# Router logits in one decoder layer: high and low weight parts as one 72-column stationary operand, product in three pieces

## What is computed

```
x = LN(alpha*x + mix)                                   # 512 x 1024
g_logit = x @ rg_w + rg_b                               # 4 groups
e_logit = x @ re_w + re_b                               # 32 experts, 8 to a group
group   = argmax(softmax(g_logit))
top 2 of the 8 experts of that group, weights renormalised, times the group's probability
y = sum over the chosen experts of  (silu(x @ gate) * (x @ up)) @ down
x = LN(alpha*x + y);  x = x + sigmoid(x @ W_g) * (p @ W_p)
```

## Time and profile before

| | us |
|---|---|
| median of 3 runs | 634.6 |
| the three runs | 635.39, 634.60, 633.86 |
| the profiled execution, its own time | 636.33 |
| its span, first to last instruction | 634.6 |
| PE busy | 602.2 (95%) |
| DVE busy | 353.9 (56%) |
| ACT busy | 182.5 (29%) |
| POOL busy | 170.6 (27%) |
| moved by DMA | 149.88 MB, mean 236 GB/s |

### The profile page before, as it was taken

The page is one execution under the profiler, slowest core; times in us unless marked ns, Lnnn a source line. Parts: engine busy times, 40 slices in busy tenths (PEclk is TensorE's granted clock), DMA queues, the critical chain, the costliest instruction groups (busy, mean ns, idle before and its releaser), DMA issues.

```text
span 634.6 us, 11747 instructions
## 1 busy us (share of the span) xinstructions
PE 602.2 (95%) x4575; PEld 435.4 (69%) x4575; DVE 353.9 (56%) x857; ACT 182.5 (29%) x360; POOL 170.6 (27%) x191
## 2 busy tenths in 40 slices
PE   8999999999999999998899999996699999978997
PEld 6768979878888778887665555564465555535885
DVE  6799994788787677869562113221111221129855
ACT  5587324344243245202101111110011111234221
POOL 2428772001010011512033332343233343111100
PEclk9999999999999999999799999997999999989999
DMA  7503241013004001399959999999999999977003
GB/s 245 220 31 150 84 170 63 1 47 154 1 2 164 36 1 68 124 390 395 380 226 367 368 418 416 420 413 421 413 418 416 416 418 415 421 307 313 0 3 135
DMA packets 29286, 149.88 MB, mean 236 GB/s; under 512 B 5993, under 2 KB 6457, under 8 KB 15273
## 3 DMA queue, kind: packets, MB, share of 16 engines
q1 hardware_dynamic: 23624, 140.65, 55.6%
q0 software_dynamic: 5600, 8.42, 3.7%
HBM read 145.23 MB, written 12.98 MB: 249 GB/s over the span
## 4 chain that ended last, share of the span: by engine, by line
PE 75%; DMA 10%; DVE 9%; issue 3%; ACT 1%; POOL 1%; SPq 0%; DVEq 0%; ACTq 0%
PE bank L2318 13%; PE bank L1945 12%; PE bank L1947 12%; PE bank L1946 12%; PE bank L2374 7%; DMA rows_x<-in_ple_gate_dram 5%; DMA slots<-in_w_exp_dram 4%; PE bank L2334 3%; PE bank L2308 2%; PE bank L2050 2%; PE bank L2065 2%; PE bank L2078 2%; PE bank L2351 1%; PE bank L2108 1%; DMA raw<-in_w_in_dram 1%
## 5 line engine op out<-in xcount | busy, mean ns | idle before, releaser
L1847 DVE COPY rows_x<-bank 128x128 f32<-128x128 f32 (+1 forms) x41 | 11.0, 267 | 175.5 <-PE bank L2366 99.9
L1945 PE MATMUL bank<-w_hi,a_hi 128*128 128x384 f32 (+1 forms) x240 | 88.2, 367 | 1.7 <-DVE a_lo L1601 1.7
L1947 PE MATMUL bank<-w_hi,a_lo 128*128 128x384 f32 (+1 forms) x240 | 86.5, 361 | 0.0
L1946 PE MATMUL bank<-w_lo,a_hi 128*128 128x384 f32 (+1 forms) x240 | 86.5, 360 | 0.0
L1945 PE MATMUL bank<-a_hi,w_hi 128*128 128x512 f32 x152 | 61.4, 404 | 1.0 <-DVE w_lo L1241 0.7
L1946 PE MATMUL bank<-a_lo,w_hi 128*128 128x512 f32 x152 | 59.4, 391 | 0.0
L1947 PE MATMUL bank<-a_hi,w_lo 128*128 128x512 f32 x152 | 59.4, 391 | 0.0
L852 POOL DMA_INDIRECT pair_dram<-rows_x,row_put x26 | 26.4, 1015 | 101.0 <-ACT rows_x L1152 101.0
L1945 PEld LDWEIGHTS bank<-w_hi,a_hi 128*128 128x128 f32 x240 | 45.2, 188 | 7.0 <-DVE a_lo L1601 2.1
L1152 ACT ACTIVATE rows_x<-bank 128x512 f32<-128x512 f32 (+1 forms) x41 | 21.3, 520 | 94.9 <-PE bank L2374 72.8
L2318 PE MATMUL bank<-raw,rows_x 128*64 128x256 f32 x416 | 47.8, 383 | 0.5 <-DVE rows_x L1816 0.5
(11 more groups left out here) (320 smaller groups left out, 1141.8 us busy)
## 6 DMA issues: line engine op xcount, KB each, us to landing
raw<-in_w_exp_dram SPq DMA_DIRECT2D x45, 1024.0 KB, 17.9
slots<-in_w_exp_dram SPq DMA_DIRECT2D x24, 1024.0 KB, 23.7
pa<-in_w_exp_dram SPq DMA_DIRECT2D x21, 1024.0 KB, 17.4
raw<-in_w_in_dram SPq DMA_DIRECT2D x18, 512.0 KB, 3.5
raw<-in_w_wide_dram SPq DMA_DIRECT2D x4, 1536.0 KB, 6.9
raw<-in_w_out_dram SPq DMA_DIRECT2D x4, 1024.0 KB, 5.9
rows_x<-in_w_exp_dram SPq DMA_DIRECT2D x4, 1024.0 KB, 15.0
raw<-pair_dram SPq DMA_DIRECT2D x8, 512.0 KB, 9.2
```

Source lines behind the costliest of these rows:

```text
L1945: t_.matmul(o, lh, rh, start=first, stop=False)
L1946: t_.matmul(o, lh, rl, start=False, stop=False)
L1947: return t_.matmul(o, ll, rh, start=False, stop=last)
```

## The change

The high and the low part of the router's weights stand side by side for each block of rows, so that one stationary operand has 72 columns. One product with `a_hi` gives high x high in rows 0 to 35 and low x high in rows 36 to 71; one with `a_lo` adds high x low and low x low. So each block takes two products instead of three. The two halves of the 72 rows are added on DVE after the transposes. The product is made in three pieces, of tokens 0 to 255, 256 to 383 and 384 to 511, each in a PSUM bank of its own, and in each piece the eight products with `a_hi` come before the eight with `a_lo`, with waits by half tile. Four idle products of 512 columns stand between the first and second piece. low_first(1) moves on DVE from ahead of mixed(3, 1) to behind norm_centre(3).

```diff
-        logit_rows = take(SEQ)[0:36, :]
+        logit_rows = take(SEQ)[0:72, :]
-        WR_N = NK * 36
+        wr_two = last_lo[:, 0:NK * 72].rearrange("p (k c) -> p k c", k=NK)
+        logit_bank = [bank[4], bank[0], bank[5]]
+        LOGIT_COLS = [slice(0, 2 * P), slice(2 * P, 3 * P), slice(3 * P, 4 * P)]
...
-                sp.wait_ge(s_rp, 2)
+                sp.wait_ge(s_rp, 3)
...
-            def copy_logits(half):
-                act.wait_ge(s_rp, half + 1)
-                c = slice(half * 2 * P, (half + 1) * 2 * P)
-                a.activation(logit_rows[:, c], bank[4][0:36, c], ACT.Copy).then_inc(s_ra, 1)
+            def copy_logits(i):
+                act.wait_ge(s_rp, i + 1)
+                c = LOGIT_COLS[i]
+                a.activation(logit_rows[:, c], logit_bank[i][0:72, 0:c.stop - c.start], ACT.Copy).then_inc(s_ra, 1)
...
-                    a.activation(last_lo[:, 0:WR_N], wr_raw.rearrange("p k c -> p (k c)"), ACT.Copy)\
-                        .then_inc(s_wrs, 1)
+                    a.activation(wr_two[:, :, 0:36], wr_raw, ACT.Copy).then_inc(s_wrs, 1)
                 if u == 5:
                     copy_logits(0)
             copy_logits(1)
+            copy_logits(2)
...
             norm_scale(2, s_ln, s_rs)
-            low_first(1)
             mixed(3, 1)
             norm_centre(3, s_ln)
+            low_first(1)
             norm_scale(3, s_ln, s_rs)
             low_first(2)
             low_first(3)
...
-            step(v.tensor_tensor(logit, bank[0][:, 0:NT * 36].rearrange("p (t c) -> p t c", t=NT),
-                                 r_bias.unsqueeze(1).broadcast_to([P, NT, 36]), ALU.add))
+            turned_logits = bank[1][:, 0:NT * 72].rearrange("p (t w c) -> p t w c", t=NT, w=2)
+            step(v.tensor_tensor(logit, turned_logits[:, :, 0, :], r_bias.unsqueeze(1).broadcast_to([P, NT, 36]),
+                                 ALU.add))
+            settle()
+            step(v.tensor_tensor(logit, turned_logits[:, :, 1, :], logit, ALU.add))
...
-            def route(half):
-                pe.wait_ge(s_x1lo, 4 * half + 4)
-                c = slice(half * 2 * P, (half + 1) * 2 * P)
+            def route_high(i):
+                c = LOGIT_COLS[i]
                 for k in range(NK):
-                    mm = three(bank[4][0:36, c], wr_hi[:, k, :], wr_lo[:, k, :], a_hi[:, k, c], a_lo[:, k, c],
-                               k == 0, k == NK - 1)
+                    if k % 4 == 0:
+                        pe.wait_ge(s_x1hi, (i + 1) * 2 + 1 + k // 4)
+                    t_.matmul(logit_bank[i][0:72, 0:c.stop - c.start], wr_two[:, k, :], a_hi[:, k, c], start=k == 0,
+                              stop=False)
+
+            def route_low(i):
+                c = LOGIT_COLS[i]
+                for k in range(NK):
+                    if k % 4 == 0:
+                        pe.wait_ge(s_x1lo, (i + 1) * 2 + 1 + k // 4)
+                    mm = t_.matmul(logit_bank[i][0:72, 0:c.stop - c.start], wr_two[:, k, :], a_lo[:, k, c],
+                                   start=False, stop=k == NK - 1)
                 mm.then_inc(s_rp, 1)
...
             pe.wait_ge(s_wrs, 2)
-            route(0)
+            pe.wait_ge(s_x1lo, 2)
+            route_high(0)
+            for _ in range(4):
+                t_.matmul(bank[0][:, :], a_hi[:, 0, 0:P], a_hi[:, 0:4, 0:P], start=True, stop=True)
+            route_high(1)
+            route_low(0)
             turn_first(3)
             turn_logits(0)
-            route(1)
+            route_low(1)
+            route_high(2)
             turn_logits(1)
+            route_low(2)
+            turn_logits(2)
             idle_products(bank[3], a_hi[:, 2, :], 25)
```

More of the change, by code:

```diff
@@ L445, in hybrid_layer @@
         GATE_PARTS = (4, 8, 12)
-        RT_GROUP, RT_SECOND = 7, 24
+        RT_GROUP, RT_SECOND = 8, 25
         TB_FIXED, TB_REST, TB_BLOCK = 9, 13, 9
@@ L1630, in _ @@
             dve.wait_ge(s_wrs, 1)
-            v.tensor_tensor(last_lo[:, WR_N:2 * WR_N], wr_raw.rearrange("p k c -> p (k c)"),
-                            last_lo[:, 0:WR_N].bitcast(F32), ALU.subtract).then_inc(s_wrs, 1)
+            v.tensor_tensor(wr_two[:, :, 36:72], wr_raw, wr_two[:, :, 0:36].bitcast(F32), ALU.subtract)\
+                .then_inc(s_wrs, 1)
             mixed(2, 0)
@@ L1669, in top @@
                 settle()
-            dve.wait_ge(s_rp, 3)
+            dve.wait_ge(s_rp, 4)
             dve.wait_ge(s_rb, 16)
             dve.wait_ge(s_rc, 20 + FIX)
-            step(v.tensor_tensor(logit, bank[0][:, 0:NT * 36].rearrange("p (t c) -> p t c", t=NT),
-                                 r_bias.unsqueeze(1).broadcast_to([P, NT, 36]), ALU.add))
+            turned_logits = bank[1][:, 0:NT * 72].rearrange("p (t w c) -> p t w c", t=NT, w=2)
[3 more added lines that the diff above has]
+            step(v.tensor_tensor(logit, turned_logits[:, :, 1, :], logit, ALU.add))
             settle()
@@ L1704, in _ @@
             v.tensor_tensor(chosen[:, :, :], one[0], one[1], ALU.add).then_inc(s_cho, 1)
-            dve.wait_ge(s_ra, 4)
+            dve.wait_ge(s_ra, 5)
             step(v.tensor_reduce(col[6], dif_g, AXX, ALU.add))
@@ L2218, in turn_tile @@
                     mm.then_inc(done, 1)
-            wr_hi = last_lo[:, 0:WR_N].rearrange("p (k c) -> p k c", k=NK)
-            wr_lo = last_lo[:, WR_N:2 * WR_N].rearrange("p (k c) -> p k c", k=NK)
             def embed(u):
@@ L2229, in embed, with turn_logits @@
                 mm.then_inc(s_pp, 1)
-            def route(half):
-                pe.wait_ge(s_x1lo, 4 * half + 4)
-                c = slice(half * 2 * P, (half + 1) * 2 * P)
+            def route_high(i):
+                c = LOGIT_COLS[i]
                 for k in range(NK):
-                    mm = three(bank[4][0:36, c], wr_hi[:, k, :], wr_lo[:, k, :], a_hi[:, k, c], a_lo[:, k, c],
-                               k == 0, k == NK - 1)
-                mm.then_inc(s_rp, 1)
[L2239 to L2244, removed]
+                    if k % 4 == 0:
[9 more added lines that the diff above has]
+                                   start=False, stop=k == NK - 1)
+                mm.then_inc(s_rp, 1)
+            def turn_logits(i):
+                pe.wait_ge(s_ra, i + 1)
+                for t in range(i + 1 if i else 0, i + 2):
+                    mm = t_.transpose(bank[1][:, t * 72:(t + 1) * 72], logit_rows[:, t * P:(t + 1) * P],
+                                      ident[0:72, 0:72])
+                if i == 2:
                     mm.then_inc(s_rp, 1)
@@ L2258, in _ @@
             turn_first(2)
-            pe.wait_ge(s_wrs, 2)
-            route(0)
-            turn_first(3)
-            turn_logits(0)
-            route(1)
-            turn_logits(1)
             def idle_products(o, m, count):
@@ L2268, in idle_products @@
                     t_.matmul(o[:, :], m[:, 0:P], m, start=True, stop=True)
+            pe.wait_ge(s_wrs, 2)
+            pe.wait_ge(s_x1lo, 2)
[4 more added lines that the diff above has]
+            route_low(0)
+            turn_first(3)
+            turn_logits(0)
+            route_low(1)
+            route_high(2)
+            turn_logits(1)
+            route_low(2)
+            turn_logits(2)
             idle_products(bank[3], a_hi[:, 2, :], 25)
```

## The result

Ten runs of the changed kernel have a median of 631.62 us (630.42 to 633.13), ten of the kernel before 635.69 us. The medians differ by 4.1 us. The ratio, taken over the runs with an interval and not as the quotient of the two medians (0.9936), is 0.9934 with a 95% interval of 0.9913 to 0.9955: 0.66% faster. The profiled execution took 631.16 us, its span 629.4; the profiled one of before took 636.33 and 634.6. So the two traces differ by 5.2 us, and the medians by 4.1. The experiments are mostly about that difference.

What follows compares the result with a forecast made beforehand. PE, at half clock in the router's product, was taken to hold back the first sorted load. Terms: 0.60 + 4.86 + 0.11 + 0.17 - 0.34 = 5.4 us; 634.6 - 5.4 = 629.2 us, range 627.8 to 632.5.

Steps and rivals of the forecast that it cites:

- The rival of an end that doesn't move: Whole kernel: the end hangs on a total of transfers which doesn't move, 634.6 us; chance 0.07.
- the late gather: Ahead of the first expert item: first gather lands 1 to 3 us late, PE waits, 630 to 632; chance 0.06.
- DVE order: low_first(1) moved back on DVE: fourth tile's scaling comes earlier without waiting for POOL, gain 0.60 us.
- Fourth tile to last low part: Router, from turn_first(3) to the last low part: stays unchanged at 2.63 us.
- The copy that I called tight: copy_logits(1) on ACT, ahead of turn_logits(1) and route_low(2): PE waits for it; costed at 0, upper bound 0.4 us.
- Products behind the last low part: End of the router's product on PE: 24 become 4, 0.49 us against 5.35, gain 4.86, of it 2.4 the clock.
- Transpose with hand-overs: From the last copy's end to the bias: one transpose at full clock, 0.32 us against 0.49, gain 0.17.
- the two clock cases at 631.7: Router: median run has no clock drop (chance 0.20), or clock still drops after the change (0.15); each gains 2.9 us.
- the clock's term of 2.4 us: route(1) in the kernel before: 5.35 us at half clock against 2.94 at full clock, counted whole as gain.
- The three times 1.5 us apart: Three known times of the kernel before: their spread doesn't exclude that other executions escape the clock drop.
- The rival at 0.15: Router: clock still drops, idle products run slow and end behind `chosen`; loss 2.5, gain 2.9, 631.7 us; chance 0.15.
- the first rival: Router: clock did not drop in the median run before, so gain is 2.9 us, 631.7; chance 0.20.

Runs made afterwards that it cites:

- the first set of experiments: Both kernels again, clock_only, and the changed kernel without its four idle products; 35 runs of the kernel before beside them have a median of 635.84 us.
- clock_only: Kernel before plus 7 idle products behind route(0) and 5 ahead of route(1); median 635.24 us, ratio 0.9983 (0.9948 to 1.0017).
- merge_only: Kernel before with 72 stationary columns, two products a block, and the second add, its order and halves kept; 636.40 us, ratio 1.0006.
- clock_look: One more trace of clock_only, nothing changed against it; traced run 634.52 us.
- before_look1: Kernel before, unchanged, first of three more traces; traced run 634.16 us.
- before_look3: Kernel before, unchanged, third of three more traces; traced run 637.30 us.
- before_look2: Kernel before, unchanged, second of three more traces; traced run 643.19 us.

## Why the prediction was right, and where it missed

*The path.* B and C carry it. Over fourteen traces the first sorted load is issued anywhere from 319.6 to 331.3 us, and from there to the end it is 309.3 to 310.6. Time saved ahead of the load arrives at the end. The traces of the changed kernel and its variants have a mean C of 310.0 (six), the others 309.6 (eight); whether 0.3 us is given back in the expert items stays open, as the spread within each is as large. The rival of an end that doesn't move falls, and so does the late gather: PE goes from its idle products into the first item without a wait in all of them.

*DVE order, 0.60.* Measured 0.59 (5.93 to 5.34), and 0.59 with only this undone. The wait for POOL is gone, as said.

*Fourth tile to last low part, unchanged at 2.63.* It is 304.24 - 301.63 = 2.61. The copy that I called tight costs nothing; PE's own work in between costs 0.05.

*Products behind the last low part.* 0.49 was forecast and the chain has 0.49. I took 0.09 us for their distance. The eight of route_low(1) are (0.71 - 0.22)/7 = 0.07 apart; in the last four the first takes 0.28 and the others about 0.22, from the first start to the last end it is 0.47, so they are some 0.08 apart, and 0.02 of hand-over makes up the 0.49. The price was laid between those of two other forms, and its bounds were worth no more than 0.1 us either way. Route(1) itself was put at 5.35 us; its rows make 309.50 + 0.41 - 304.58 = 5.33. Copy: 0.27 against 0.28. Transpose with hand-overs, from the copy's end to the bias: 0.37 against 0.32. Second add: 0.34, as forecast.

*The sum.* A fell by 16.19 - 10.49 = 5.70, less 0.34 for the add is 5.36, against 5.4. The profiled execution was to take 630.9 us and took 631.16; it came to norm_scale(2) 0.32 us later than the one of before.

*The median.* The forecast of 629.2 was 2.4 us too low; the measured 631.62 is inside the range of 627.8 to 632.5, which I had drawn so wide in order to hold the two clock cases at 631.7. Two steps missed. The first is the base: the three runs known had a median of 634.6, ten have 635.69 and the 35 beside the first set of experiments 635.84; that is 1.1 us. The second, the other 1.3 us, is the clock's term of 2.4 us, which the sum took whole because the one trace had it. I gave 0.20 to a median run without the drop, as one of two states. The traces show neither state as the rule: 5.3 us are gained where the drop is whole, 2.9 where it is absent, 4.45 (29.57 - 25.12) where it is partial, and the median gained 4.1. The term should have been a mean over executions. The five traces alone would make it 1.75 us ((3 x 2.4 + 1.54)/5), the medians less: 4.1 - 2.9 = 1.2, and 0.6 by clock_only. The three times 1.5 us apart, which I read as not excluding it, were the sign. The share is not settled. One more sign is in the 35 runs of before: 13 lie at 633.65 to 634.85 us and 16 at 635.47 to 636.34, with none between, and the mean granted clock over the whole run is 0.988 or more in twelve of the 13 and 0.980 to 0.987 in the 16. That would fit runs without and with the drop. But the groups are 1.5 us apart and not 2.4, the mean clock counts drops anywhere in the kernel, and the 12 and 17 runs of the other sets have no such gap, so it is not shown.

*The clock in the changed kernel* held in all six traces of it and its variants with the reordered products, without the four idle products too. The rival at 0.15 didn't come, but what I described there was seen in merge_only: an early bias and a clock that is down make `places` late. It and the first rival both stood at 631.7, and the median came out at 631.62; the number alone could not have told them or a partial gain apart, the traces do. The Trainium skill (TensorE: Matmul & The Clock Gate, Part 4) says that transposes don't count as busy in the way of products. The kernel before, with transposes alone in the gap (1.33 us of 3.6), lost the clock in four of five traces, merge_only in its one, and clock_only and clock_look, with products put around the same transposes, kept it, which agrees. before_look1 kept it over the same transposes, so they don't decide it alone. A gap of which PE is simply idle for most would look the same, and no run here had transposes in place of products in a full stretch, which would test it. The runs of the changed kernel lie within 2.7 us (630.42 to 633.13), those of the kernel before, the outliers aside, within some 4.

## What to carry to other kernels

Before you price a stretch at a low clock, take several traces of it: a drop that follows a gap in TensorE's work can come in one execution and not in the next, and its term is a mean. Fewer products can lose as much as they save if what they leave is a gap: what worked here was to put the products into the gap, high parts first and in pieces, so that four short ones and not 24 stand behind the last input. Where idle products pad a wait on the path, they turn a low clock into a late result; check that they still end before what they wait for.

## What had not been expected

The same binary program has the clock down over its router for about 7 us, for about half of that, or not at all (before_look3, before_look2, before_look1), and up to 2.4 us of the time with it. A shorter router product went with a longer drop: in the trace of merge_only from about 302.8 to 313.1 us, in that of the kernel before from 303.8 to 310.6. A plain float32 product of 72 x 36 takes two instructions on TensorE and 0.41 us against 0.28 for a float32 transpose of 72 columns.
